# One transformer layer on one core: four V buffers, a scratch tile of its own, and the output projection's rows and squares placed anew

## What is computed

```python
xn = rms_norm(x, attn_norm)
q, k, v, xl, yg, gl = jnp.split(xn @ w_in, IN_SPLITS, axis=-1)     # 1024 x 5632
q, k = partial_rope(rms_norm(q, q_norm), pos), partial_rope(rms_norm(k, k_norm), pos)
attn_branch = windowed_attention_with_sinks(q, k, v) @ w_attn_out
lru_branch = (rg_lru(conv4(xl)) * gelu(yg)) @ w_lru_out
g_a, g_b = jnp.split(sigmoid(gl), 2, axis=-1)
x = x + (g_a * attn_branch + g_b * lru_branch) @ w_o
gate, up = jnp.split(rms_norm(x, ffn_norm) @ w_gate_up, 2, axis=-1)
x = x + (silu(gate) * up) @ w_down
```

## Time and profile before

| | |
|---|---|
| three runs | 1670.12, 1673.92, 1674.09 us; median 1673.92 us |
| profiled execution: its own time | 1669.02 us |
| its span | 1667.2 us |
| PE busy | 1615.4 us, 97% of the span |
| DVE, POOL, ACT busy | 1009.1, 944.5, 625.7 us (61, 57, 38%) |
| granted PE clock, mean of the span | 0.989 |

### The profile page before, as it was taken

One profiled execution on the slowest core, in us unless ns is written; L12 is line 12 of the kernel. 1 busy time (PEld: TensorE's weight loads), 2 busy tenths in 40 slices (PEclk: granted clock), 3 DMA queues, 4 the chain that ended last, 5 costly groups with the idle time before them and its releaser, 6 DMA issues. The chain is left out here.

```text
span 1667.2 us, 28466 instructions
## 1 busy us (share of the span) xinstructions
PE 1615.4 (97%) x11270; PEld 1536.9 (92%) x11270; DVE 1009.1 (61%) x1718; ACT 625.7 (38%) x1294; POOL 944.5 (57%) x685
## 2 busy tenths in 40 slices
PE   7999998999999999999898999999999999999999
PEld 4899998989989898898897989999999999998998
DVE  6676555855545555857888787333333334869595
ACT  5535551253343425414334343333333333433232
POOL 4545552313212230568875709777777777786876
PEclk9999999999999999999999999999999999999999
DMA  5111222313122130364343412222242222473643
GB/s 182 47 51 64 64 76 88 91 56 113 61 96 69 67 118 31 117 246 169 134 151 103 155 59 84 78 77 78 77 181 78 77 79 76 146 281 117 240 145 147
DMA packets 73032, 182.09 MB, mean 109 GB/s; under 512 B 15092, under 2 KB 26676, under 8 KB 72260
## 3 DMA queue, kind: packets, MB, share of 16 engines
q1 hardware_dynamic: 52228, 160.35, 27.7%
q10 hardware_dynamic: 20672, 19.93, 3.8%
HBM read 131.23 MB, written 49.28 MB: 108 GB/s over the span
## 5 line engine op out<-in xcount | busy, mean ns | idle before, releaser
L597 PE MATMUL bank<-xh,wsh 128*128 128x264 f32 x2170 | 622.7, 287 | 21.5 <-POOL wsl L573 8.3
L597 PE MATMUL bank<-xh,wsl 128*128 128x264 f32 x2170 | 618.8, 285 | 0.0
L597 PE MATMUL bank<-xl,wsh 128*128 128x264 f32 x2170 | 618.2, 285 | 0.0
L597 PEld LDWEIGHTS bank<-xh,wsh 128*128 128x128 f32 x2170 | 410.4, 189 | 25.1 <-issue 15.5
L597 PEld LDWEIGHTS bank<-xl,wsh 128*128 128x128 f32 x2170 | 410.6, 189 | 0.3
L597 PEld LDWEIGHTS bank<-xh,wsl 128*128 128x128 f32 x2170 | 410.6, 189 | 0.0
L597 PE MATMUL bank<-acth,wh 128*128 128x352 f32 x960 | 318.7, 332 | 6.0 <-POOL wl L524 3.6
L597 PE MATMUL bank<-acth,wl 128*128 128x352 f32 x960 | 314.8, 328 | 0.0
L597 PE MATMUL bank<-actl,wh 128*128 128x352 f32 x960 | 313.6, 327 | 0.0
L522 POOL TENSOR_SCALAR wh<-wraw 128x512 fp32r<-128x512 f32 (+1 forms) x100 | 72.4, 724 | 396.1 <-PE bank L597 374.4
L573 POOL TENSOR_TENSOR wsl<-praw,wsh 128x512 fp32r<-128x512 f32 (+1 forms) x157 | 243.8, 1553 | 82.8 <-ACT wsh L1212 82.7
(11 more groups left out here) (179 smaller groups left out, 2308.7 us busy)
## 6 DMA issues: line engine op xcount, KB each, us to landing
praw<-in_weights SPq DMA_DIRECT2D x34, 1024.0 KB, 4.9
wraw<-in_weights SPq DMA_DIRECT2D x52, 512.0 KB, 3.3
h_scratch<-ev SPq DMA_DIRECT2D x44, 264.0 KB, 2.0
acc<-h_scratch SPq DMA_DIRECT2D x4, 2112.0 KB, 12.7
ev<-x_scratch SPq DMA_DIRECT2D x6, 1056.0 KB, 5.0
spare<-x_scratch SPq DMA_DIRECT2D x6, 1056.0 KB, 5.0
praw<-in_weights SPq DMA_DIRECT2D x8, 768.0 KB, 5.2
ta_scratch<-tg ACTq DMA_DIRECT2D x24, 176.0 KB, 1.9
```

What stands on the lines that cost most here:

```text
L597: return nc.tensor.matmul(*args, **kw)
```

## The change

The V tile has four buffers in place of two, so a copy waits for the fourth last store; the stores of the last V job and of `tail` stand behind the second K job. The activation part of `LRU_OUT` that lay in `spare` gets a tile of its own, `t2raw`, in the place of `xl6` (whose low part waits for product 6 of pair 0). So SP loads res[1] for pair 1 at pair 0, and `load_pair(3)` stands ahead of `load_x`. At pair 4 the `ta_scratch` rows are loaded ahead of the store of pair 3's result. In `OUT` pair 9 takes its rows from res[1], loaded at pair 8 beside pair 8's. Since that is `spare`, `ssum` is zeroed at pair 10, and the squares move: those of pairs 8 and 9 are made in pair 10, those of pair 10 at products 0 and 1 of pair 11, and those of pair 11, as before, in its own steps. Pair 10 thus has 16 squares and additions (eight of pair 8 ahead of its `u2`, `u4`; eight of pair 9 at r = 3 to 6), pair 11 also 16.

```diff
@@ res_loads
-        return {LRU_OUT: (q % 2,), ATTN_OUT: (0, 1), OUT: (0,), GATE_UP: ()}.get(t, ((q - PHASE_FIRST[DOWN]) % 2,))
+        return {LRU_OUT: (q % 2,), ATTN_OUT: (0, 1), OUT: (int(q == PHASE_FIRST[OUT] + 1),), GATE_UP: ()}.get(t, ((q - PHASE_FIRST[DOWN]) % 2,))
+def squares_at(p, r):
+
+    i = p - PHASE_FIRST[OUT]
+    if i < 2:
+        return ()
+    if r < 2:
+        return tuple((PHASE_FIRST[OUT] + 2 * i - 4, 2 * r + k) for k in range(2))
+    return ((PHASE_FIRST[OUT] + 2 * i - 3, r - 3),) if r > 2 else ()
@@ build: tiles
-            vst = tensor(s, "vst", [P, 2, KVH * HD])
+            vst = tensor(s, "vst", [P, 4, KVH * HD])
-        for k in range(4, PRODUCTS):
+        for k in range(4, 6):
             x_slot(k)
+        xh.append(tensor(ctx, "xh6", [P, KQ, HALF], f32r))
+        with ExitStack() as raw:
+            t2raw = tensor(raw, "t2raw", [P, KQ, HALF])
+        xl.append(tensor(ctx, "xl6", [P, KQ, HALF], f32r))
-            return fifth if t == LRU_OUT else quarter(t, 0, 1)
+            return t2raw[:, :, :] if t == LRU_OUT else quarter(t, 0, 1)
@@ scalar
-                if t >= 2:
-                    act.wait_ge(v_stored[t % 2], 16 * (t // 2))
-                f(vst[:, t % 2, :], bank[job.bank][:, 0:KVH * HD], ACT.Copy).then_inc(free[job.bank], 1)
+                if t >= 4:
+                    act.wait_ge(v_stored[t % 4], 16 * (t // 4))
+                f(vst[:, t % 4, :], bank[job.bank][:, 0:KVH * HD], ACT.Copy).then_inc(free[job.bank], 1)
                 if t >= 1:
                     store_v(t - 1)
-            store_v(8)
-            act.wait_ge(tail_done, 6 * GROUPS)
-            act.dma_start(tail_out, tail[:, :, :]).then_inc(stored, 16)
-
...
                 qk_copy(j // 6 * 6, j % 6, (kgain, qgain)[j // 6])
+                if j == 1:
+                    store_v(8)
+                    act.wait_ge(tail_done, 6 * GROUPS)
+                    act.dma_start(tail_out, tail[:, :, :]).then_inc(stored, 16)
@@ scalar: squares
                     if j >= 3:
                         act.wait_ge(ssum_done, j - 2)
-                    row = res[0][:, m, :] if p == X_FIRST[OUT] else acc[:, 2 * (p - PHASE_FIRST[OUT]) + m, :]
+                    elif j == 0:
+                        act.wait_ge(acc_copied, 2)
+                        act.wait_ge(zero_done, 1)
+                    row = acc[:, 2 * (p - PHASE_FIRST[OUT]) + m, :]
...
-                if t == OUT and r >= 3:
-                    x1_square(p, r - 3, (c22_done, c11_done, c12_done, c21_done)[r - 3],
-                              (1, 0, 0, 1)[r - 3], (1, 0, 1, 0)[r - 3])
+                if t == OUT:
+                    for q, i in squares_at(p, r):
+                        x1_square(q, i)
@@ vector
+            def add_squares(p, r):
+                for q, i in squares_at(p, r):
+                    for n in range(2):
+                        add_square(8 * (q - PHASE_FIRST[OUT]) + 2 * i + n)
+
...
                 if t == OUT and r >= 4:
-                    for n in range(2):
-                        add_square(8 * i + 2 * (r - 4) + n)
+                    add_squares(p, r - 1)
                     if r == 6:
-                        for n in range(2):
-                            add_square(8 * i + 6 + n)
+                        add_squares(p, 6)
...
-                if p == PHASE_FIRST[OUT]:
+                if p == PHASE_FIRST[OUT] + 2:
+                    for done in (c22_done, c11_done, c12_done, c21_done):
+                        dve.wait_ge(done, 2 * nth(p))
                     V.memset(ssum, 0.0).then_inc(zero_done, 1)
+                if t == OUT:
+                    add_squares(p, 0)
+                    add_squares(p, 1)
@@ sync
-                    load_res(0, tiles(tb_dram, 0))
+                    for b in range(2):
+                        load_res(b, tiles(tb_dram, b))
                     return
-                if p == 1:
-                    x_unused(LRU_OUT)
-                    load_res(1, tiles(tb_dram, 1))
                 store_mb(p - 1)
...
-                if p == 1:
-                    load_x(ATTN_OUT)
...
                 if i == 0:
+                    sp.wait_ge(mb_stored[0], 32)
+                    load_res(0, tiles(ta_dram, i))
                     store_mb(p - 1)
-                    for b in range(2):
-                        sp.wait_ge(mb_stored[b], 32)
-                else:
-                    sp.wait_ge(merged, MERGED_LRU + 4 * i)
+                    sp.wait_ge(mb_stored[1], 32)
+                    load_res(1, tiles(mb_dram, i))
+                    return
...
                 if i == 0:
                     sp.wait_ge(merged, MERGED_LRU + 4 * PAIRS[ATTN_OUT])
-                elif i == 1:
+                    for b in range(2):
+                        load_res(b, x_in[:, 2 * b:2 * b + 2, :])
+                    return
+                if i == 1:
                     sp.wait_ge(acc_copied, 2)
-                else:
+                    load_res(0, x_in[:, 4:6, :])
+                elif i == 3:
                     sp.wait_ge(c21_done, 2 * nth(p - 1) + 2)
-                load_res(0, x_in[:, 2 * i:2 * i + 2, :])
-                if i:
-                    store_x1(p - 1)
+                    load_res(0, x_in[:, 6:8, :])
+                store_x1(p - 1)
...
                 if p + 2 < N_PAIRS:
                     load_pair(p + 2)
+                if p == 1:
+                    load_x(ATTN_OUT)
```

More of the change, by code:

```diff
@@ L454, in build @@
         one_done, b_done, h_done, prod_done = sem("lru_first_mult"), sem("lru_b"), sem("lru_h"), sem("lru_product")
-        v_stored, kv_stored, cs_loaded = [sem(f"v_stored{i}") for i in range(2)], sem("kv_stored"), sem("rope_loaded")
+        v_stored, kv_stored, cs_loaded = [sem(f"v_stored{i}") for i in range(4)], sem("kv_stored"), sem("rope_loaded")
         ss_done, copied, std_done = sem("k_sumsq"), sem("qk_copied"), sem("k_std")
@@ L1037, in store_v @@
                 if t < 8:
-                    act.dma_start(v_dram[t * P:(t + 1) * P, :], vst[:, t % 2, :]).then_inc(v_stored[t % 2], 16)
+                    act.dma_start(v_dram[t * P:(t + 1) * P, :], vst[:, t % 4, :]).then_inc(v_stored[t % 4], 16)
                 else:
-                    act.dma_start(v_dram[SEQ:T, :], vst[P - DEC:P, t % 2, :]).then_inc(v_stored[0], 16)
+                    act.dma_start(v_dram[SEQ:T, :], vst[P - DEC:P, 0, :]).then_inc(v_stored[0], 16)
                     act.dma_start(vs_out[WINDOW - DEC:WINDOW, :], vst[P - DEC:P, 0, :]).then_inc(stored, 16)
                 if t == 7:
-                    act.dma_start(vp_out[:, :], vst[:, 1, :]).then_inc(stored, 16)
+                    act.dma_start(vp_out[:, :], vst[:, 3, :]).then_inc(stored, 16)
             vjobs = []
@@ L1111, in _ @@
                 if j == 6:
-                    act.wait_ge(v_stored[0], 16 * 5)
-                    act.wait_ge(v_stored[1], 16 * 4)
+                    act.wait_ge(v_stored[0], 16 * 3)
+                    for i in range(1, 4):
+                        act.wait_ge(v_stored[i], 16 * 2)
                     act.wait_ge(stored, 16 * 3)
                 qk_copy(j // 6 * 6, j % 6, (kgain, qgain)[j // 6])
+                if j == 1:
+                    store_v(8)
+                    act.wait_ge(tail_done, 6 * GROUPS)
+                    act.dma_start(tail_out, tail[:, :, :]).then_inc(stored, 16)
                 if 1 <= j < 7:
@@ L1243, in copy_back, with x1_square @@
                 f(acc[:, 0:2, :], res[0], ACT.Copy).then_inc(acc_copied, 1)
-            def x1_square(p, i, done, m, h):
+            def x1_square(p, i):
+                done, m, h = ((c22_done, 1, 1), (c11_done, 0, 0), (c12_done, 0, 1), (c21_done, 1, 0))[i]
                 for n in range(2):
@@ L1606, in part_low @@
                 dve.wait_ge(xhi_done, nth_high(t, k))
+                if t == LRU_OUT and k == 6:
+                    dve.wait_ge(mm_done, ended(0, 6))
                 n = chunks_of(t)
@@ L1709, in first_sums, with row_in @@
                     stt(u4(par, n), bank[BANKS[1][n]][:, 0:QB], scale, u2(par, n), ALU.mult, ALU.add).then_inc(u4_done, 1)
-            def rows_in(p):
-                for b, n in res_loads(p).items():
-                    dve.wait_ge(res_in[b], n)
+            def row_in(p, b):
+                dve.wait_ge(res_in[b], res_loads(p)[b])
             def combine_gated(p, r):
@@ L1725, in combine_gated @@
                 if r == 4:
-                    rows_in(p)
+                    row_in(p, b)
                 for n in range(2):
@@ L1749, in combine_gated @@
                         x_unused(t)
+                    row_in(p, 1)
                     dst = half if i == 0 else acc[:, 2 * i + m, toks(h)]
@@ L2081, in _ @@
             sp.wait_ge(x1_stored, 16 * PAIRS[OUT])
+            sp.wait_ge(v_stored[0], 16 * 3)
+            for i in range(1, 4):
+                sp.wait_ge(v_stored[i], 16 * 2)
             sp.wait_ge(stored, 16 * (4 + 3))
```

5 lines of the change are left out of this document (2 added, 3 removed).

## The result

| | before | changed |
|---|---|---|
| runs | 1670.12 to 1678.12 us, 4 | 1647.17, 1650.00, 1651.04, 1653.27 us |
| median | 1674.01 us | 1650.52 us |
| profiled execution: time, span | 1669.02, 1667.2 us | 1647.17, 1645.4 us |
| granted PE clock, mean of the span | 0.989 | 0.993 |

The ratio of the runs is 0.9866, interval 0.9847 to 0.9885: 22.4 us faster (19 to 26). 1652 was forecast, in a range of 1643 to 1662. One execution in this document, the profiled one of `qsb_on_before`, ran at a mean clock of 0.565 (2598.09 us) and is left out of its median.

The account below looks back on a forecast made before the run. Four stretches of PE waits and low clock were traced to transfers late through a buffer or queue place. 5.1 + 8.7 + 1.1 + 10.6 - 3.5 = 22.0 us off 1669.0 gives 1647.0 profiled, 1652 median; range 1643 to 1662.

Parts of the forecast that it names:

- Step 1: V stage: copies lose their store waits, 7.1 us available less 1.9 of a new bank 0 wait; gain 5.1.
- Steps 2 and 3: Pairs 2 to 4: late rows and weights come earlier, gain 8.7 us; pairs 4 and 5: DVE arrives earlier, gain 1.1.
- step 2: Pairs 2 to 4: early res[1] and weights ahead of load_x remove DVE's 3.0 and POOL's 3.2 us waits; gain 8.7.
- Rival C: SP's new order makes the first attention parts wait for load_x behind weights, about 4 us: 1656; chance 0.08.
- Step 4: Pairs 8 and 9: earlier rows and 16 additions fewer on DVE end PE's waits and half clock; gain 10.6 us.
- Step 5: Pairs 10 to 12: moved squares delay pair 11's high and low parts, then pair 12's weights; loss 3.5 us.
- rival D: DVE bounds pairs 10 and 11, every addition at 1.525 us beside POOL: 6.6 us slower, 1680; chance 0.03.
- A: Rope chain has unseen slack and pair 12 is not held more: +2.0 and +3.5 us, 1646.5; chance 0.2.
- B: Additions beside POOL hold PE in pairs 10 and 11, c22 late: 5.2 us more, 1658; chance 0.2.
- E: Other causes close behind V, rows and weights return 17 us as other waits: 1670, within 0.3%; chance 0.04.

Follow-up runs that it names:

- qsb_on_before: The kernel before with three buffers for the scaled copies of the K and Q jobs, nothing of the change: 1667.54 us, ratio 0.9979.
- v_alone: The kernel before with only the four V buffers and the later stores: 1672.09 us, ratio 0.9993.
- qsb_three: The changed kernel with three buffers in place of two for the scaled copies of the K and Q jobs: 1643.46 us, ratio 0.9824.
- three_mends: The changed kernel with the third scaled-copy buffer, Q sums spread between dense matmuls and pair 12's weights scaled first: 1638.12 us, ratio 0.9803.
- rows_alone: The kernel before with t2raw, early res[1], pair 3's weights ahead of load_x and pair 4's gate rows ahead of the store: 1663.42 us, ratio 0.9938.
- load_x_first: The changed kernel with the attention's activations loaded ahead of pair 3's weights again, res[1] still early: 1651.64 us, ratio 0.9885.
- out_alone: The kernel before with only the OUT stage of the change: 1662.78 us, ratio 0.9945.
- rows_late: The changed kernel with pair 9's rows in res[0] again, loaded after pair 8's result is copied out, squares still moved: 1662.14 us, ratio 0.9944.
- sums_spread: The changed kernel with each group's 17 small Q-sum products put one by one behind 17 successive dense matmuls: 1652.17 us, ratio 0.9872.
- adds_double: The changed kernel with each addition of squares followed by a maximum of the same two tiles: 1668.38 us, ratio 0.9974.

## Why the prediction was right

The total was met, 1652 against 1650.5, but two of its steps were wrong, by some 4 and 3.5 us, and cancelled. That the total came within 2 us is luck; steps 2 to 4, 20.4 of its 22.0 us, are not.

**Step 1, the V stage: 5.1 forecast, about 1 measured.** The 7.1 us available were there. The new wait for bank 0 came at its place (in before the matmul of 320.24) with 0.9 us in place of 1.9, and the same chain held PE a second time, 2.64 us at the Q sums, which the step did not look at: 3.5 in place of 1.9. That the copies into `vst` wait for no store was wrong: one still waits 6.78 us, but no longer holds PE. What failed most is the sentence that stretches at half clock elsewhere would only shift by a few us either way, "in the spread". They answer to this edit: 13.5 us more at the lower level in `v_alone`, 3.5 more in the first trace of the changed kernel, where V kept 2 us. `qsb_three` and `three_mends` point to how: PE idle just ahead of a row of small products. The term belonged in the sum: from the Q sums to the end of pair 0 the same seven traces lose 2 to 8 us of PE's lead.

**Steps 2 and 3: 9.8 forecast, 8.7 from pair 0's end to pair 7's in the trace, 10.4 in `rows_alone`.** Right in size; within step 2 the reason given for POOL's half, the 4.2 MB ahead of the weights, fell with `load_x_first`. The early res[1] carries both halves. Rival C falls with it: no first attention part waits for its load, in either order.

**Step 4: 10.6 forecast, 10.4 in the trace over pairs 8 and 9, 9.2 (5.7 to 12.6) in `out_alone`.** Right in size. The 14 us of additions taken from DVE, and the earlier copy, had a small part: `rows_late` has both, gains 2.9 us on before in pairs 8 and 9, and gives more than that back ahead of pair 12.

**Step 5: 3.5 lost forecast, none measured (from the end of pair 9 to pair 12's first product 0.5 gained in one trace, 0.8 lost in the other, within these two in `load_x_first`, `sums_spread` and `qsb_three`).** The failed step is "late by what two or three additions more take". In pair 11 of the changed kernel, POOL and then DVE:

```profile
922.35 1.50 POOL L586 TENSOR_TENSOR wsl<-praw,wsh 128x512 fp32r<-128x512 f32 x1
926.63 1.29 POOL L586 TENSOR_TENSOR wsl<-wsum,wsh 128x512 fp32r<-128x512 f32 x1 [2.79 <-ACT wsh L1226]
...
921.16 5.38 DVE L1713 TENSOR_TENSOR spare<-spare 128x264 f32<-128x264 f32 x9
```

As squares hold ACT, POOL waits 2.79 us for a high part, and nine additions take 5.38 us, 0.60 each. All 32 of them (busy and mean; then least, median and most in ns):

```profile
L1713 DVE TENSOR_TENSOR spare<-spare 128x264 f32<-128x264 f32 x32 | 18.3, 636 | 6.7 <-ACT spare L1271 6.7
...
L1713 DVE TENSOR_TENSOR spare<-spare x32: 418/425/1529, 901.6 to 942.0; 128x264 f32<-128x264 f32 x32
```

0.64 for 0.87 on the mean, 0.425 for 0.677 in the median. Laid over POOL's timeline, 20 of the 32 additions of before overlap a POOL instruction (1.14 us on the mean), and 9 of the changed kernel's (1.18 us); of the others none is longer than 0.434 us. So the extra work paid part of itself by silencing its competitor, which I had used against rival D and not in my own sum; that this makes up the whole 3.5 us is not shown. The margin is thin, as `adds_double` and the 3.8 us in `rows_late` show; why the two traces of the changed kernel differ by 1.3 us at `praw` is open. The Trainium skill's rule ("SBUF — State Buffer", SBUF: two separate sides) agrees with the two ends, 0.42 where POOL is idle and up to 1.53 beside it.

Of the rivals, A came half true: pair 12 is held hardly more than before (PE waits 1.27 and 2.6 us for `praw` in the two traces where it waited 1.55), which the prediction itself had named as A's sign, and this offsets step 1; its other half, a rope chain with slack, did not. B's wait for c22's bank stands in no pair; where additions do hold PE, in `adds_double`, it is `u4`, to which the prediction had given cover. D and E are out.

## What to carry over

When an edit makes PE arrive early at a chain that another engine sets, look at the buffer between them first: with the edit in place one more tile was worth 7 to 10 us, the edit itself 1.2. A stall is not only its idle time; ask what PE does right behind it, and if those are products of few columns, price the clock as well. And a load that is late in a queue may be late because of what waits ahead of it, not what moves ahead of it.

## What the runs showed of the hardware

At the starts of attention groups 2 to 4, behind 17 products of two columns made in a row in about 4 us, the granted clock fell to the lower level in 28 of 33 cases, although PE counts as busy throughout; with the same products between dense matmuls in one of six. At group 1 PE was idle for 2.6 to 2.8 us just ahead of these products in eight traces, and 7 to 13.5 us at the lower level followed, whether they stood in a row (seven traces) or spread (`sums_spread`). Without that idle time it was 0 to 7 us with the row (four traces) and none in the one with the products spread.

Additions of two SBUF tiles of 264 columns on DVE took 0.42 to 0.43 us while POOL was idle and, where they overlapped a POOL instruction, 1.14 us on the mean in before and 1.18 in the changed kernel, at most 1.53.
